# Two norms' sums of squares placed two by two among dense matmuls, and their factors spread later, in a two-layer hybrid decoder step

## The reference

```
u   = rms_norm(h) @ w_in                      # columns cut into four groups
ssd = rms_norm(SSD(u) * silu(z), w)           # one norm over 256 channels
ret = group_norm(Retention(u)) * silu(g)      # centred, per head of 64
gla = head_rms_norm(GLA(u)) * silu(r)         # per head of 64
lru = RG_LRU(u) * gelu(y)                     # a linear recurrence over time
h  += concat[ssd, ret, gla, lru] @ w_out
h  += (silu(n @ w_gate) * (n @ w_up)) @ w_down,  n = rms_norm(h)
```

## Time and profile before

| | us |
|---|---|
| median of 3 executions | 1318.83 (1317.6 to 1319.07) |
| profiled execution, its own time | 1318.84 |
| span of its trace, first to last instruction | 1317.0 |
| TensorE matmuls busy | 1288.6 (98%) |
| VectorE busy | 856.3 (65%) |
| ScalarE busy | 705.5 (54%) |
| GpSimd busy | 293.6 (22%) |
| mean granted TensorE clock | 0.989 of full speed |

### The profile page before, as it was taken

One profiled execution on the slowest core, in us unless ns is written; L12 is line 12 of the kernel. 1 busy time (PEld: TensorE's weight loads), 2 busy tenths in 40 slices (PEclk: granted clock), 3 DMA queues, 4 the chain that ended last, 5 costly groups with the idle time before them and its releaser, 6 DMA issues.

```text
span 1317.0 us, 26928 instructions
## 1 busy us (share of the span) xinstructions
PE 1288.6 (98%) x10781; PEld 1236.4 (94%) x10781; DVE 856.3 (65%) x1697; ACT 705.5 (54%) x1209; POOL 293.6 (22%) x248
## 2 busy tenths in 40 slices
PE   7999999999999999999999999999999999999996
PEld 7988898999999999999999898899999999999996
DVE  6845765478854785378757566656788358835864
ACT  7626455576632664265653374546766247624651
POOL 1101101112252224224411010001123412341250
PEclk9999989999999999999999998999999999999998
DMA  8855745657744784476567575457487347734741
GB/s 274 215 123 139 177 98 118 133 114 169 172 140 97 168 172 141 98 169 184 147 139 164 122 167 122 99 118 173 106 178 181 105 103 174 196 101 106 163 129 68
DMA packets 63388, 189.73 MB, mean 144 GB/s; under 512 B 7585, under 2 KB 8865, under 8 KB 63265
## 3 DMA queue, kind: packets, MB, share of 16 engines
q0 software_dynamic: 27936, 67.12, 31.0%
q1 hardware_dynamic: 30672, 111.95, 26.8%
q10 hardware_dynamic: 4656, 8.95, 2.3%
HBM read 180.33 MB, written 5.43 MB: 141 GB/s over the span
## 4 chain that ended last, share of the span: by engine, by line
PE 73%; DVE 10%; DVEq 5%; ACT 5%; DMA 3%; issue 3%; ACTq 0%
PE bank L1649 47%; PE bank L1678 17%; DVEq L1492 2%; DMA raw<-weights 2%; DVE up L1523 1%; DMA wl<-weights 1%; DVE tz L1519 1%; DVE wsum L1420 1%; PE bank L1593 1%; DVEq L1419 1%; ACT wh L552 1%; ACT tz L838 1%; ACT wl L551 1%; DVE tz L1495 1%; PE bank L1970 1%
## 5 line engine op out<-in xcount | busy, mean ns | idle before, releaser
L523 POOL DMA_DIRECT2D wl<-weights x194 | 168.1, 867 | 884.0 <-ACT wl L551 873.6
L1649 PE MATMUL bank<-xh,wh 128*128 128x272 f32 x800 | 243.4, 304 | 8.2 <-DVE xl L950 7.6
L552 ACT ACTIVATE wh<-raw 128x512 fp32r<-128x512 f32 (+1 forms) x243 | 197.8, 815 | 86.3 <-PE bank L1649 79.0
L1649 PE MATMUL bank<-xl,wh 128*128 128x272 f32 x800 | 233.9, 292 | 0.0
L1649 PE MATMUL bank<-xh,wl 128*128 128x272 f32 x800 | 233.7, 292 | 0.0
L551 ACT ACTIVATE wl<-raw 128x512 fp32r<-128x512 f32 (+1 forms) x192 | 145.8, 760 | 119.0 <-PE bank L1649 107.0
L1678 PE MATMUL bank<-xh,wh 128*128 128x272 f32 x704 | 202.9, 288 | 0.6 <-DVE tz L1507 0.3
L1678 PE MATMUL bank<-xl,wh 128*128 128x272 f32 x704 | 202.2, 287 | 0.0
L1678 PE MATMUL bank<-xh,wl 128*128 128x272 f32 x704 | 202.2, 287 | 0.0
L552 ACT ACTIVATE wh<-wsum 128x512 fp32r<-128x512 f32 x176 | 105.2, 622 | 126.9 <-DVE wsum L1420 88.8
L1649 PEld LDWEIGHTS bank<-xh,wh 128*128 128x128 f32 x800 | 154.8, 194 | 19.4 <-issue 17.4
(11 more groups left out here) (404 smaller groups left out, 3019.1 us busy)
## 6 DMA issues: line engine op xcount, KB each, us to landing
raw<-weights SPq DMA_DIRECT2D x202, 512.0 KB, 6.2
wl<-weights POOLq DMA_DIRECT2D x132, 256.0 KB, 5.5
wl<-weights POOLq DMA_DIRECT2D x62, 512.0 KB, 7.2
h<-x SPq DMA_DIRECT2D x4, 544.0 KB, 5.9
y<-h SPq DMA_DIRECT2D x4, 544.0 KB, 2.7
rv<-rk ACTq DMA_DIRECT2D x8, 136.0 KB, 2.6
tz<-rq ACTq DMA_DIRECT2D x8, 136.0 KB, 5.6
S<-s_ssd ACTq DMA_DIRECT2D x2, 512.0 KB, 6.7
```

Of the source, the lines that this page charges most:

```text
L523: nc.gpsimd.dma_start(wl[:, place(j)], weights[n][:, lo:lo + width], accum_op=ALU.add).then_inc(lo_added[BLOCK0[j] % RING], 16)
L552: a(wh[:, place(j)], whole, ACT.Copy).then_inc(hi_done, 1)
L1649: ins = mm(bank_, wt[:, at:at + P], xx[:, half], start=(i == 0 and pass_ == 0), stop=(i == len(ks) - 1 and pass_ == 2))
```

## The change

The ten sums of squares of the GLA norm no longer follow half 35 as one block. `unit_half` takes a function `after` that it calls behind each k-step; in half 36, and for the SSD norm in half 41, it issues the two sums of one chunk after each of the first five k-steps. The sums of the retention norm stay one block. The spreading of the factors moves a slot later for GLA (37, 38, 39) and two slots later for SSD (42, 43). VectorE's and ScalarE's parts of `ssd_stat` move from slot 39 to 40, those of `gla_stat` stay in 35. The first operand of the recurrence (`lru_out(0)`, slot 41) so comes ahead of the two SSD operands (slot 43), and the counts and `OUT_K` follow.

```diff
-OUT_K = [0, 1, 6, 7, 4, 5, 2, 3]
+OUT_K = [6, 0, 1, 7, 4, 5, 2, 3]
...
-    at_slot(40 + _i, "ssd_norm", _i)
+    at_slot(42 + _i, "ssd_norm", _i)
...
-    at_slot(36 + _i, "gla_norm", _i)
+    at_slot(37 + _i, "gla_norm", _i)
 at_slot(38, "ssd_squares")
-at_slot(39, "ssd_stat")
+at_slot(40, "ssd_stat")
...
-                        high(0, G_SSD, 0, xbc[:, 0, :])
-                        high(1, G_SSD, 1, xbc[:, 1, :])
+                        high(1, G_SSD, 0, xbc[:, 0, :])
+                        high(2, G_SSD, 1, xbc[:, 1, :])
...
-                    "lru_out": lambda t: high(2 + t, G_LRU, t, tz[:, t, :]),
+                    "lru_out": lambda t: high(3 * t, G_LRU, t, tz[:, t, :]),
...
-                        low(0, G_SSD, 0, xbc[:, 0, :])
-                        low(1, G_SSD, 1, xbc[:, 1, :])
+                        low(1, G_SSD, 0, xbc[:, 0, :])
+                        low(2, G_SSD, 1, xbc[:, 1, :])
...
-                    low(2 + t, G_LRU, t, tz[:, t, :])
+                    low(3 * t, G_LRU, t, tz[:, t, :])
...
-                def unit_half(u, half, rhs, ks, before=None, steps=None):
+                def unit_half(u, half, rhs, ks, before=None, steps=None, after=None):
...
-                    if steps[-1] == len(ks) - 1:
-                        ins.then_inc(dense_done, 1)
+                        if (i, pass_) == (len(ks) - 1, 2) and steps[-1] == i:
+                            ins.then_inc(dense_done, 1)
+                        if after is not None:
+                            after(i)
...
-                def head_stat(i):
+                def head_stat(i, c):
 
-                    pe.wait_ge(n_sq.sem, n_sq.at(layer, i + 1))
-                    if i:
-                        pe.wait_ge(n_used.sem, n_used.at(layer, 5))
-                    for c, off, n in CH:
-                        for t in range(2):
-                            at = 4 * c + 2 * t
-                            ins = mm(M[4][0:n, at:at + 2], sq[:, t, off:off + n], cst("pair"), start=True, stop=True)
-                    ins.then_inc(n_mm.sem, 1)
+                    if c == 0:
+                        pe.wait_ge(n_sq.sem, n_sq.at(layer, i + 1))
+                        if i:
+                            pe.wait_ge(n_used.sem, n_used.at(layer, 5))
+                    _, off, n = CH[c]
+                    for t in range(2):
+                        at = 4 * c + 2 * t
+                        ins = mm(M[4][0:n, at:at + 2], sq[:, t, off:off + n], cst("pair"), start=True, stop=True,
+                                 skip_group_check=True)
+                    if c == SAMPLE:
+                        ins.then_inc(n_mm.sem, 1)
...
-                def ssd_stat(_=None):
+                def ssd_stat(c):
...
+                    def norm_sums(k):
+                        if k < 5:
+                            if s == 36:
+                                head_stat(0, k)
+                            else:
+                                ssd_stat(k)
                     if s > 1:
-                        unit_half(s // 2, s % 2, x_operand, range(KT))
+                        unit_half(s // 2, s % 2, x_operand, range(KT), after=norm_sums if s in (36, 41) else None)
```

More of the change, by code:

```diff
@@ L1960, in ret_b_, with ret_stat @@
                     ins.then_inc(ret_b.sem, 1)
-                def head_stat(i):
-                    pe.wait_ge(n_sq.sem, n_sq.at(layer, i + 1))
-                    if i:
-                        pe.wait_ge(n_used.sem, n_used.at(layer, 5))
-                    for c, off, n in CH:
-                        for t in range(2):
-                            at = 4 * c + 2 * t
-                            ins = mm(M[4][0:n, at:at + 2], sq[:, t, off:off + n], cst("pair"), start=True, stop=True)
-                    ins.then_inc(n_mm.sem, 1)
+                def head_stat(i, c):
[10 more added lines that the diff above has]
+                        ins.then_inc(n_mm.sem, 1)
+                def ret_stat(_=None):
+                    for c in range(5):
+                        head_stat(2, c)
                 def head_spread(out, c, t):
@@ L1992, in gla_norm_ @@
                     ins.then_inc(n_spread.sem, 1)
-                def ssd_stat(_=None):
[L1995 to L2001, removed]
+                def ssd_stat(c):
+                    if c == 0:
+                        pe.wait_ge(n_sq.sem, n_sq.at(layer, 2))
+                        pe.wait_ge(n_used.sem, n_used.at(layer, 3))
+                    _, off, n = CH[c]
+                    for t in range(2):
+                        ins = mm(M[4][0:n, c:c + 1], sq[:, t, off:off + n], ones[:],
+                                 start=(t == 0), stop=(t == 1), skip_group_check=True)
+                    if c == SAMPLE:
+                        ins.then_inc(n_mm.sem, 1)
                 def ssd_norm_(i):
@@ L2031, in _ @@
                     "gla_a": gla_a_, "gla_b": gla_b_, "ret_a": ret_a_, "ret_b": ret_b_,
-                    "gla_stat": lambda: head_stat(0), "gla_norm": gla_norm_, "ssd_stat": ssd_stat,
-                    "ssd_norm": ssd_norm_, "centre": centre, "ret_stat": lambda: head_stat(2), "ret_norm": ret_norm_,
+                    "gla_norm": gla_norm_,
+                    "ssd_norm": ssd_norm_, "centre": centre, "ret_stat": ret_stat, "ret_norm": ret_norm_,
                 }
```

## The result

The changed kernel is slower: 1325.46 us (median of 18 executions) against 1319.12 (18), ratio 1.0047 with a 95% interval of 1.0034 to 1.0060. The forecast was 1318.7 and no change, with 1322.0 as its upper end. Its executions also scatter more: 1320 to 1333 us, those of before 1315 to 1321. One execution of each was far slower than the rest (1396.44 and 2080.65 us) and is left out of the ratio and of these two ranges.

What follows compares the result with a forecast made beforehand. TensorE, busy 98%, was taken as the bound, paying only where it waits, runs at half clock or does needless work. Layer 0 +0.6 and layer 1 -0.7 us gave -0.1 on 1318.84: 1318.7 us, 80% range 1315.0 to 1322.0.

Steps and rivals of the forecast that it cites:

- (a): GLA sums inside half 36: four more returns to dense work cost 0.1 us; `ret_b(0)` at 168.26 instead of 169.82.
- (b): `gla_norm` one slot later: `ret_b(0)` to `ret_b(1)` takes 10.17 us instead of 10.82; TensorE's wait grows to about 1.1 us.
- (c): `ret_b(1)` to `ret_b(2)`: VectorE sets 11.86 us; `ret_b(2)` at 190.29 instead of 193.62, new TensorE wait of 1.6 us.
- (d): `ret_b(2)` to `ret_a(4)`: SSD sums come in, the wait before `ret_a(4)` goes; 16.46 us instead of 14.89.
- (e): `ret_a(4)` to `centre`: `ssd_norm(1)` adds 2.6 us on VectorE; 14.77 us instead of 12.38, new wait of 2.1 us.
- Rival A: VectorE in slots 43 to 46 not late, no wait before `centre`: -4.9 us, 1313.9; chance 0.25 in full or most.
- C: Rival: spreading the sums in halves 36 and 41 does not keep the clock, four falls stay: +6.2 us, 1324.9; chance 0.08.
- (f): The recurrence's output first among the operands ahead of the output units, and `OUT_K`: 0 us.
- the clock: The 17.0 us at half clock behind the GLA and SSD sums cost 7.7 us, all given back as waits.
- Layer 0 59.11, layer 1 60.44: Times of the kernel before from `ret_a(0)` to `centre`, compared with 59.74 us for the changed kernel: together -0.1 us.
- Work outside does not change: Outside `ret_a(0)` to `centre`: nothing changes; no matmul, byte or DMA is added or removed.
- rival B: Clock still falls at the new waits before `ret_b(2)` and `centre`: 1.55 us each, two falls +3.0 us, 1321.7; chance 0.17.

Runs made afterwards that it cites:

- before_a: The kernel before, no edit, profiled again for the places of its slow stretches: 1318.87 us.
- after_again: The changed kernel, no edit, profiled and timed again against the kernel before on its own chip: 1324.82 us, ratio 1.0034.
- after_c: The changed kernel, no edit, profiled again for the places of its slow stretches: 1326.66 us, one execution.
- scan_late: The changed kernel with the second recurrence scan, `lru_scan(1)`, moved from slot 38 to 39: 1319.40 us, ratio 1.0011 to the kernel before.
- sums_block: The changed kernel with the sums as blocks again behind half 35 and half 40, other moves kept: 1328.40 us, ratio 1.0074 to the kernel before.
- sums_only: The kernel before with only the two-by-two sums, GLA in half 36, SSD in half 40, other slots and order as before: 1314.40 us, ratio 0.9963.
- sums_only_2: The kernel before with only the two-by-two sums, repeated on another chip: 1313.35 us, ratio 0.9973 to the kernel before.
- ssd_early: The kernel before with two-by-two sums, SSD sums in half 40, and the GLA factors one slot later (37 to 39): 1335.85 us, ratio 1.0153.

## Why the prediction was wrong

Steps (a) to (e) were right for what they say of the chain. (a): 0.23 us for the four more returns, inside its bounds of 0 to 0.43, above the 0.1 taken. (b) and (c): within 0.1 us, the scan on VectorE holds `ret_b` as said; only TensorE's wait in (b) is 0.76 us instead of 1.1. (d): the wait before `ret_a(4)` is gone and ScalarE's copy of V is the limit by 0.19 us. (e): 2.45 against 2.6 us, a wait of 1.91 against 2.1 (its own figures give 14.77 - 12.38 = 2.4; the spread of `ssd_norm(1)`, which now stands in this stretch too, 0.24 us in the changed trace, was taken off without a word). Rival A is out, C is out. (f), the order of the operands, had no run of its own.

The step that failed is the clock: that all 17.0 us at half clock, 7.7 us of time, would come back and nothing be lost elsewhere. The executions close this sum. At full clock the way from `ret_a(0)` to `centre` takes 59.67 us instead of about 55.97 (57.52 in layer 0 of `before_a`, with one unit there, less 1.55), so +7.4 us in the two layers; the forecast had +7.6. Of that 6.7 are waits of TensorE: 4.4 us a layer (0.76 + 1.54 + 0.19 + 1.91) against 1.1. Time at half clock fell by 4.0 us (28.8 to 24.8), not by 17.0, worth 1.7 us at 0.41 to 0.44 us each and not 7.7. 7.4 - 1.7 = +5.7 us, and the mean of the 29 executions is 5.7 us above that of the kernel before timed beside them (1324.77 against 1319.08). On the chip of `after_again` alone it is 6.4 us less at half clock, 7.4 - 2.8 = +4.6, and +4.6 measured.

The profiles show where the rest of the 17.0 us went. Two terms of the sum were wrong.

*"Layer 0 59.11, layer 1 60.44": the state compared with.* The 17.0 us at half clock behind the sums were read from one execution and taken as fixed. They are not: the four profiles of the kernel before have 119.55, 116.55, 119.50 and 116.59 us for the two layers, mean 118.05. The changed kernel's have 119.35, 119.33, 123.68 and 119.33, mean 120.42. This term is +2.4 us instead of -0.1; of it 1.5 is the base and 1.1 the one long fall in `after_c`.

*"Work outside does not change": rival B, undervalued.* Outside these stages the profiles of before have 1.25 falls in the mean, those of the changed kernel 2.5, the difference being about the four behind `centre`. 1.25 x 1.55 = +1.9 us. B had been named with its mechanism, its price and both places, but with 0.17 and as all or nothing at two falls. The wait of 1.9 us gave one fall of this kind in each of four profiles, and the wait before `ret_b(2)` a fall of three units in one of them.

Together +4.3 us, against medians that differ by 6.3 and 5.2. The eight profiled executions differ by +4.2 in the mean (1323.97 against 1319.78), but they come from different chips, so that this agreement proves little. How often each place falls is known only from four profiles a kernel. That the wait before `centre` brings the clock down is shown by the place: with 1.9 us a fall begins within 2 us of `centre`'s start in 5 of 12 layers (the changed kernel 4 of 8, `scan_late` 1 of 2, `sums_block` 0 of 2), with 3.8 us in 2 of 2, and without a wait in none of 16. What decides in which execution it falls stays open.

The Trainium skill ("TensorE: Matmul & The Clock Gate", "Why this matters for your kernels") has the rule that idle gaps between matmul bursts bring the engine back to half clock. It means longer gaps than the 1.6 and 2.1 us to which the prediction applied it. The runs agree where the gap is 3.8 us (a fall in both layers) and show more: at 1.9 us it depends on the execution. Its price, half of the throttled time (Terms), is above the 0.41 to 0.44 us per us that the executions show; my 1.55 of 3.4 (0.46) lies between.

## What to carry to other kernels

A clock fall read from one profile is a draw, not a property of the program: take several profiles of the kernel before, or the mean clock of many executions, before counting on getting it back. Where an engine chain is as tight as here, moving a stage later on the engine that feeds TensorE buys idle time on TensorE (6.7 us of waits here), and idle time can have a second price in the clock. Spread the sums where that adds no wait: the sums two by two gained 0.3 to 0.4% by themselves, and the later factors and outputs gave back more than that.

## What the runs showed of the hardware

- The same program loses its clock at different places in different executions: behind the GLA sums of layer 0 in two of four, at the layer's end in three of four.
- A fall of 3.4 us cost 1.5 to 1.6 us: from `ret_a(0)` to `centre` in layer 0 the kernel before takes 59.11 and 59.07 us with two units and 57.52 and 57.54 with one.
- A dense half thinned with short matmuls ran at full clock in eight of eight stretches of `sums_only` and `sums_only_2`. Once the clock has fallen in one it stays down through the half: 10.2 us in `after_c`, 10.2 and 13.7 us in `ssd_early`, against 3.4 us, at times 6.8, for a fall in dense work.
- Twenty short matmuls cost 2.09 us as a block and 2.3 us in five groups of four (`ret_b(0)` at 6.61 us less 1.23 and 3.07). Four of them between dense matmuls take 0.36 us, and the first dense matmul behind them 0.21 instead of 0.12 (starts at 165.06, 165.42 and 165.63 in the changed kernel).
